# A gated recurrence's 256 x 256 matrices, multiplied as rounded high and low terms in place of full fp32

## What is computed

```python
def rg_lru_branch(xr, conv_w, conv_b, w_x, b_x, w_a, b_a, a_param):
    xc = lax.conv_general_dilated(xr, conv_w[:, None, :], ...) + conv_b     # 4 taps, causal
    xh = xc.reshape(B, S, LRU_HEADS, LRU_HEAD_DIM)                          # 4 heads of 256
    gate_x = jax.nn.sigmoid(jnp.einsum('bshi,hij->bshj', xh, w_x) + b_x).reshape(B, S, C)
    gate_a = jax.nn.sigmoid(jnp.einsum('bshi,hij->bshj', xh, w_a) + b_a).reshape(B, S, C)
    log_a = -LRU_C * gate_a * jax.nn.softplus(-a_param)
    a = jnp.exp(log_a)
    b = jnp.sqrt(-jnp.expm1(2.0 * log_a)) * (gate_x * xc)
    h_t = a_t * h_(t-1) + b_t
```

## Time and profile before

| | us |
|---|---|
| median of three runs | 2767.15 |
| lowest and highest | 2765.8, 2768.48 |
| the profiled execution | 2769.62 |
| its span in the profile | 2767.8 |

### The profile page before, as it was taken

The page is one execution under the profiler, slowest core; times in us unless marked ns, Lnnn a source line. Parts: engine busy times, 40 slices in busy tenths (PEclk is TensorE's granted clock), DMA queues, the critical chain, the costliest instruction groups (busy, mean ns, idle before and its releaser), DMA issues.

```text
span 2767.8 us, 38496 instructions
## 1 busy us (share of the span) xinstructions
PE 2721.0 (98%) x16358; PEld 2253.6 (81%) x16358; DVE 1441.4 (52%) x2360; ACT 1059.7 (38%) x1604; POOL 36.2 (1%) x62
## 2 busy tenths in 40 slices
PE   9988999999999999999999999999999999999998
PEld 7787788888887778888888888886888788888887
DVE  6834476643625666765336443374644444654433
ACT  5534454332424664433234222245433422432221
POOL 0001200000000000000000000001000000000000
PEclk9999999999999999999999999999999999999999
DMA  4200122222521002322222222236222222232232
GB/s 160 90 4 3 49 90 98 99 97 93 162 102 36 2 1 79 110 94 99 99 84 99 99 99 93 99 116 130 81 87 80 77 94 96 87 104 97 94 99 69
DMA packets 68686, 238.85 MB, mean 86 GB/s; under 512 B 7800, under 2 KB 10360, under 8 KB 68004
## 3 DMA queue, kind: packets, MB, share of 16 engines
q1 hardware_dynamic: 62256, 220.80, 23.8%
q10 hardware_dynamic: 6260, 15.59, 2.5%
HBM read 228.23 MB, written 6.03 MB: 85 GB/s over the span
## 4 chain that ended last, share of the span: by engine, by line
PE 93%; DVE 3%; ACT 3%; issue 1%; DMA 0%; POOL 0%; ACTq 0%; DVEq 0%
PE psum L155 23%; PE psum L157 23%; PE psum L156 23%; PE psum L1330 3%; PE psum L1297 2%; PE psum L1317 2%; PE psum L843 2%; PE psum L201 2%; PE psum L202 1%; PE psum L209 1%; PE psum L1840 1%; PE psum L1976 1%; PE psum L177 1%; PE psum L178 1%; PE psum L176 1%
## 5 line engine op out<-in xcount | busy, mean ns | idle before, releaser
L155 PE MATMUL psum<-x_hi,w_hi 128*128 128x512 f32 x2128 | 844.7, 397 | 0.6 <-DVE w_lo L130 0.6
L157 PE MATMUL psum<-x_hi,w_lo 128*128 128x512 f32 x2128 | 829.1, 390 | 0.0
L156 PE MATMUL psum<-x_lo,w_hi 128*128 128x512 f32 x2128 | 828.2, 389 | 0.0
L130 DVE TENSOR_TENSOR w_lo<-raw,w_hi 128x1024 fp32r<-128x1024 f32 x409 | 499.9, 1225 | 390.4 <-ACT w_hi L123 390.4
L123 ACT ACTIVATE w_hi<-raw 128x1024 fp32r<-128x1024 f32 x409 | 427.9, 1050 | 304.7 <-DMA raw<-w_down 83.4
L155 PEld LDWEIGHTS psum<-x_hi,w_hi 128*128 128x128 f32 x2128 | 399.6, 188 | 90.7 <-issue 5.6
L156 PEld LDWEIGHTS psum<-x_lo,w_hi 128*128 128x128 f32 x2128 | 399.7, 188 | 86.3 <-issue 5.0
L157 PEld LDWEIGHTS psum<-x_hi,w_lo 128*128 128x128 f32 x2128 | 399.4, 188 | 84.1
L155 PE MATMUL psum<-h_hi,w_hi 128*128 128x512 f32 x616 | 239.6, 389 | 0.0
L156 PE MATMUL psum<-h_lo,w_hi 128*128 128x512 f32 x616 | 239.6, 389 | 0.0
L157 PE MATMUL psum<-h_hi,w_lo 128*128 128x512 f32 x616 | 239.6, 389 | 0.0
(11 more groups left out here) (412 smaller groups left out, 3313.0 us busy)
## 6 DMA issues: line engine op xcount, KB each, us to landing
raw<-w_up SPq DMA_DIRECT2D x88, 512.0 KB, 3.3
raw<-w_down SPq DMA_DIRECT2D x44, 512.0 KB, 3.3
raw<-w_f1up SPq DMA_DIRECT2D x44, 512.0 KB, 3.3
raw<-w_f2up SPq DMA_DIRECT2D x44, 512.0 KB, 3.3
raw<-w_qkv SPq DMA_DIRECT2D x36, 512.0 KB, 3.3
raw<-w_blend SPq DMA_DIRECT2D x28, 512.0 KB, 3.3
raw<-w_f1down SPq DMA_DIRECT2D x22, 512.0 KB, 3.3
raw<-w_f2down SPq DMA_DIRECT2D x22, 512.0 KB, 3.2
```

What stands on the lines that cost most here:

```text
L130: dve.tensor_tensor(self.w_lo[u % SLOTS][:], self.raw[u % SLOTS][:], self.w_hi[u % SLOTS][:].bitcast(F32), ALU.subtract).then_inc(self.lo_ ...
L155: pe.matmul(bank[:], hi, x_hi[:, kk], start=kk == 0, stop=False)
L156: pe.matmul(bank[:], hi, x_lo[:, kk], start=False, stop=False)
L157: mm = pe.matmul(bank[:], lo, x_hi[:, kk], start=False, stop=kk == kt - 1)
```

## The change

The gate's operands are split like those of the carrying product. For each head j there is a split of four high parts on ScalarE (Scan.split_act: the two tiles of xc, and 512 columns each of wx and wa) and of four low parts on VectorE (Scan.split_dve), both at h = 4j. The low parts of the matrices take the matrices' own place (wx_lo over wx, wa_lo over wa). A gate becomes 12 matmuls of rounded operands in place of 4 in fp32. TensorE waits for the four low parts (split_lo) in place of the taps.

The split operands lie over memory that is free at that time: for even j in rounded, over sq0 to r; for odd j, xc's parts lie in tiles 4 to 7 of e_rounded, over the later half of lru_e, and the matrices' high parts in r's place and in tile 8 of z2_even. Split 0 therefore waits for all eight tiles of the convolution (tap3), split 1 for rel_rv (made) and for its write to DRAM (written), splits 2 and 3 for the gates that read the same memory two heads earlier (pair).

```diff
--- before.py
+++ after.py
@@ -1814,6 +1814,39 @@
             sem(f"lru_{n}") for n in ("pair", "gx", "ga", "ex", "th", "own", "q", "root", "b", "h"))
         self.made, self.written = sem("rel_made"), sem("rel_written")
         self.ones = sem("dl_ones")
+        self.split_hi, self.split_lo = sem("lru_split_hi"), sem("lru_split_lo")
+
+    def operands(self, j):
+        k, mem = self.k, self.mem
+        r, e = k.rounded, mem.e_rounded
+        if j % 2 == 0:
+            return [r[:, 0], r[:, 1]], [r[:, 2], r[:, 3]], (r[:, 4], r[:, 5])
+        return [e[:, 4], e[:, 5]], [e[:, 6], e[:, 7]], (r[:, 6], mem.z_rounded[:, 8])
+
+    def split_act(self, act, j):
+        mem, (xh, _, wh) = self.mem, self.operands(j)
+        if j == 0:
+            act.wait_ge(mem.loaded, 32)
+            act.wait_ge(self.tap3, KD)
+        if j == 1:
+            act.wait_ge(self.made, 2)
+            act.wait_ge(self.written, 16)
+        if j >= 2:
+            act.wait_ge(self.pair, 2 * j - 2)
+        for kt in range(2):
+            act.activation(xh[kt], mem.xc[:, 2 * j + kt], ACT.Copy).then_inc(self.split_hi, 1)
+        for hi, w in zip(wh, (mem.wx, mem.wa)):
+            act.activation(hi, w[:, 4 * P * j:4 * P * (j + 1)], ACT.Copy).then_inc(self.split_hi, 1)
+
+    def split_dve(self, dve, j):
+        mem, (xh, xl, wh) = self.mem, self.operands(j)
+        for kt in range(2):
+            dve.wait_ge(self.split_hi, 4 * j + kt + 1)
+            dve.tensor_tensor(xl[kt], mem.xc[:, 2 * j + kt], xh[kt].bitcast(F32), ALU.subtract).then_inc(self.split_lo, 1)
+        for m, (hi, w, lo) in enumerate(zip(wh, (mem.wx, mem.wa), (mem.wx_lo, mem.wa_lo))):
+            c = slice(4 * P * j, 4 * P * (j + 1))
+            dve.wait_ge(self.split_hi, 4 * j + 3 + m)
+            dve.tensor_tensor(lo[:, c], w[:, c], hi.bitcast(F32), ALU.subtract).then_inc(self.split_lo, 1)
 
     def gate(self, h):
 
@@ -1827,17 +1860,21 @@
         t = self.gate(h)
         if t is not None:
             if t == 0:
-                pe.wait_ge(mem.loaded, 32)
                 k.tile_kept(pe, self.source, 5)
             if t == 1:
                 pe.wait_ge(self.made, 2)
             if t >= 2:
                 pe.wait_ge(self.ga, t - 1)
-            pe.wait_ge(self.tap3, t // 2 * 2 + 2)
-            for bank, w in zip(self.gate_banks(t), (mem.wx, mem.wa)):
+            j = t // 2
+            xh, xl, wh = self.operands(j)
+            pe.wait_ge(self.split_lo, 4 * j + 4)
+            for bank, hi, w in zip(self.gate_banks(t), wh, (mem.wx_lo, mem.wa_lo)):
                 for kt in range(2):
-                    o = ((t // 2 * 2 + kt) * 2 + t % 2) * P
-                    mm = pe.matmul(bank, w[:, o:o + P], mem.xc[:, t // 2 * 2 + kt], start=kt == 0, stop=kt == 1)
+                    c = slice((kt * 2 + t % 2) * P, (kt * 2 + t % 2 + 1) * P)
+                    low = w[:, 4 * P * j:4 * P * (j + 1)][:, c]
+                    pe.matmul(bank, hi[:, c], xh[kt], start=kt == 0, stop=False)
+                    pe.matmul(bank, hi[:, c], xl[kt], start=False, stop=False)
+                    mm = pe.matmul(bank, low, xh[kt], start=False, stop=kt == 1)
             mm.then_inc(self.pair, 1)
 
     def powers(self, act, t):
@@ -1857,6 +1894,8 @@
             act.wait_ge(self.pair, t + 1)
             act.activation(mem.gx[:, t], one, ACT.Sigmoid, bias=k.v("b_x", t)).then_inc(self.gx, 1)
             act.activation(mem.ga[:, t], two, ACT.Sigmoid, bias=k.v("b_a", t)).then_inc(self.ga, 1)
+        if h in (0, 4, 8, 12):
+            self.split_act(act, h // 4)
         if h == 2:
             act.wait_ge(self.made, 2)
             row = mem.rv[:].rearrange("p (a n) -> p a n", a=1).to_broadcast([12, P, SKEW])
@@ -1873,6 +1912,8 @@
                 self.tangents(act, j)
 
     def dve(self, dve, h):
+        if h in (0, 4, 8, 12):
+            self.split_dve(dve, h // 4)
         if 11 <= h < 15:
             self.squares(dve, h - 11)
 
@@ -2277,6 +2318,8 @@
             k.w_lo = [sb(f"w_lo{j}", [P, UB * P], F32R, s) for j in range(SLOTS)]
         k.raw = [sb(f"raw{j}", [P, UB * P]) for j in range(SLOTS)]
         k.w_hi = [sb(f"w_hi{j}", [P, UB * P], F32R) for j in range(SLOTS)]
+        with ExitStack() as s:
+            k.rounded = sb("sq_to_r_rounded", [P, 7, T], F32R, s)
         k.sq = [sb(f"sq{j}", [P, T]) for j in range(2)]
         k.ht = [sb(f"ht{j}", [P, T]) for j in range(2)]
         k.acc, k.ln, k.r, k.rn = (sb(n, [P, T]) for n in ("acc", "ln", "r", "rn"))
@@ -2342,11 +2385,15 @@
                 sb("lru_e_first", [P, 4, T], stack=s2)
                 B.pick, B.rmask, B.rv, B.table = (sb(f"rel_{n}", shape, stack=s2) for n, shape in (
                     ("pick", [32, SKEW]), ("mask", [12, SKEW]), ("rv", [12, SKEW]), ("table", [32, 12])))
+            with ExitStack() as s2:
+                B.e_rounded = sb("lru_e_rounded", [P, KD, T], F32R, s2)
             B.e = sb("lru_e", [P, KD, T], stack=s)
             with ExitStack() as s2:
                 B.m_hi, B.m_lo = sb("m_hi", [P, KD, T], F32R, s2), sb("m_lo", [P, KD, T], F32R, s2)
             with ExitStack() as s2:
                 last = [sb(f"dil_last{j}", [P, T], stack=s2) for j in range(7)]
+            with ExitStack() as s2:
+                B.z_rounded = sb("z2_even_rounded", [P, 9, T], F32R, s2)
             z_even = sb("z2_even", [P, 9, T], stack=s)
             with ExitStack() as s2:
                 B.z = [z_even, sb("z2_odd", [P, 9, T], stack=s2)]
@@ -2358,6 +2405,8 @@
                 B.lru_small = sb("lru_small", [P, 4, KD], stack=s2)
             with ExitStack() as s2:
                 B.xc = sb("lru_xc", [P, KD, T], stack=s2)
+                with ExitStack() as s3:
+                    B.wx_lo, B.wa_lo = sb("lru_wx_lo", [P, 2 * D], F32R, s3), sb("lru_wa_lo", [P, 2 * D], F32R, s3)
                 B.wx, B.wa = sb("lru_wx", [P, 2 * D], stack=s2), sb("lru_wa", [P, 2 * D], stack=s2)
         with ExitStack() as s:
             B.gx = sb("lru_gx", [P, KD, T], stack=s)
```

## The result

The changed kernel takes **2824.8 us** (median of four runs, 2824.4 to 2825.6) against 2766.5 for the kernel before, measured beside it (median of four): a ratio of 1.021, 95% interval 1.0198 to 1.0223, **58.3 us slower**. The forecast was 2825.

The account below looks back on a forecast made before the run. TensorE, without idle time in this stretch, was taken as the bound. Stalls 15.2 + 43.2, restarts 2 x 2.6, less 5.6 saved, gave +58.0 on 2767.15: 2825 us; bounds 2818 to 2830, 8 in 10 for 2814 to 2831.

Parts of the forecast that it names:

- The matmuls: In each of eight gates, 12 rounded matmuls take 2.73 us against 3.43 in fp32: 0.70 saved a gate, 5.6 in all.
- The first wait: Ahead of gate 0, TensorE waits for split 0, which ScalarE starts only after all eight convolution tiles: 15.2 us stall.
- The second wait: Ahead of gate 2, split 1 waits for the bias rows' write, issued at gate 0's end, taking 53.3 us: 43.2 us stall.
- The clock: After both stalls TensorE restarts at half rate: 2.6 us lost each, bounds 0 to 3.4.
- The other gates: At gates 4 and 6 the split comes some 0.7 us early, costing nothing; bound 0 to 1.4 us for both.
- The sum: Over the whole kernel, 15.2 + 43.2 + 2 x 2.6 - 5.6 = +58.0 us, giving 2825 us.
- A: Rival at the bias rows' write: alone in the queues it takes 24.8 us, so +29.5, 2797 us; chance 0.06.
- B: Rival after this stretch: TensorE is not the bound, the delay is all given back, leaving the 5.6 saving: 2761.5 us; chance 0.01.
- C: Rival at the gates: rounded matmuls run at fp32's pace, 55 us lost instead of 5.6 won: 2885 us; chance 0.02.
- D: Rival at the restarts: both waits but no clock loss, +52.8, 2820 us; chance 0.12.

Follow-up runs that it names:

- The last run: Changed kernel with splits 0 and 1 on other tiles, dealt out within xr, and bias rows on every fourth of 45 partitions: 2760.0 us, ratio 0.998 to the kernel before.
- The same-place run: Changed kernel without waiting for the write; split 0, still at h = 0, has tiles over gx and waits for two convolution tiles, not eight: 2779.4 us.
- The early issue: Changed kernel with the write of the bias rows issued at h = 0, ahead of split 0, instead of at h = 2: 2811.3 us.
- the spread rows: Changed kernel with the 12 bias rows on every fourth of 45 partitions instead of 12 neighbouring ones, same bytes: 2797.7 us, ratio 1.0111.
- the filled stalls: Changed kernel with 64 and 195 fp32 matmuls on constant ones ahead of the waits of gates 0 and 2: 2821.6 us, ratio 1.0202.
- inside xr: Changed kernel with splits 0 and 1 on tiles over ga, gx and lru_e, dealt out one operation a tile within xr: 2768.0 us, ratio 1.0005.
- without the write's wait: Changed kernel with all four splits on the tiles over sq to r, so nothing waits for the bias rows' write: 2781.5 us, ratio 1.0055.

## Why the prediction was right

*The matmuls.* 0.70 us a gate was forecast; a warm gate measures 2.72 against 3.43, 0.71. The last run shows all of it, 5.4 to 5.6 us.

*The first wait.* 15.2 forecast, 15.10 measured. But its reason was half wrong: I put it to the tiles laid over sq to r, which make the split wait for all taps. The same-place run took that away and 14.8 us stayed. The step that failed is "which ScalarE starts only once tap3 has reached 8", given as what delays the split: without that wait ScalarE started 2.5 us sooner, but VectorE's differences, behind the last taps in VectorE's own order, only 0.3.

*The second wait.* 43.2 forecast, 43.63 measured, with the mechanism as told: issue with gate 0's end, landing, split, gate 2. The write was 53.9 us, in place of 53.3, and inside the range of 52.0 to 54.5. Its two parts were each off and nearly cancelled: forecast were 2.7 us ahead of the packets and 50.6 of packets; measured are 1.5 ahead of them, 52.0 of packets and 0.4 from the last of them to ScalarE's release. The early issue (11 us sooner, 11.2 us less wait) and the spread rows (25.0 us shorter, 25.0 less wait: 18.61 in place of 43.63) show that the stall's end hangs on the write and on nothing else.

*The clock.* The level was right, the price too high for this run: 2 x 2.6 forecast, 1.8 and 1.6 measured by the gates' lengths, some 3 us by the filled stalls. The mis-sized step is "nearer that row than zero": the kernel's start ran 6.7 us at half rate, these restarts 3.1 and 3.6. But the price is not a constant. Measured the same way (the gate's length less 2.72), it was 1.6 and 1.9 with the early issue, 2.0 in the same-place run, 2.3 inside xr, 2.5 without the write's wait and 2.5 twice with the spread rows. So 2.6 stands at the upper end of what restarts here cost, and which value a run gets no trace explains.

*The other gates.* 0.7 us of slack forecast. In the trace after, the last difference of split 2 ends at 1952.52 and gate 4 starts at 1953.34: 0.8 us, no wait. In the runs with the slow write and without the long stall that did not always hold: gate 4 waited 1.1 us in two of them and gate 6 5.1 us inside xr, where ScalarE had been held by a load that ran beside the write. That the long stall let such loads land first is an argument from these runs. The prediction's bound of 1.4 for both gates would not have covered the 5.1.

*The sum.* 58.0 forecast; the terms as measured give 56.5, the traces 56.7, the medians 58.3. That the forecast met the median to 0.2 us is partly luck: 1.8 too much on the clock against 1.6 that the traces do not show, and a median before that lay 0.7 lower than the one the sum was put on.

*The rivals.* A (a short write) fell: from issue to ScalarE's release it took 53.8 to 53.9 us in the four runs with the slow write and a gate that waited on it, with few loads beside it. Its last packet came 54.2 us after the issue in the kernel before and 55.3 and 55.4 in the two runs with splits inside xr and the slow write, where weight loads ran beside it all along. B (given back later) fell: the waits after 1960 are those of before. C fell by the gates' 2.72. D (no clock loss) is what the filled stalls made, and it was worth 3 us and not 5.

## What to carry to other kernels

A wait for memory to come free costs where it stands in each engine's order, so ask first when the engine reaches the instruction and only then what it waits for: removing a wait without moving its instruction gave 0.3 us, moving it as well took the whole 15 us away. When a wait on a long transfer is moved ahead, price the whole transfer from its issue, and look at what the engine would have to prepare behind the wait. And before a saving on the bounding engine is booked, look for waits that are just met (1.4 us here): they take it back. Rows that a long DMA reads can be laid on partitions further apart with the same bytes, which took 25 us off this write.

## What the runs showed of the hardware

A DMA that reads 12 neighbouring partitions of SBUF took 53.8 to 53.9 us for 3840 KB, and 28.9 us from 12 partitions four apart. While the slow one runs, weight loads of 512 KB land after 15 to 19 us in place of 3.3:

```profile
raw<-w_qkv SPq DMA_DIRECT2D x1, 512.0 KB, 19.4
```

(DMA issues of the changed kernel in 1880 to 1885.) Beside the quicker write they took 10.3 to 10.8 us.

After stalls of 15 and 44 us TensorE ran at the half clock for 3.6 and 3.1 us of dense matmuls, after 5.1 us of idle time (the splits inside xr) for some 4.4, where the kernel's start took 6.7. Over the nine gates of rounded matmuls that stood behind a stall of 5 to 44 us, in six traces, it was 3.1 to 5.3 us: the longest, 5.3, stood behind stalls of 15 and 19, the shortest, 3.1, behind 15 and 44. With the stall filled by matmuls (the run on the clock) there was none.
